# Attention with undivided probabilities, turned on TensorE by a product with a scaled unit matrix

## What is computed

```python
def memory_cross_attention(q_mem, k_mem, v_mem):
    s = jnp.einsum('bshd,bmhd->bhsm', q, k_mem).astype(jnp.float32) * (HEAD_DIM ** -0.5)
    p = jax.nn.softmax(s, axis=-1).astype(v_mem.dtype)
    return jnp.einsum('bhsm,bmhd->bshd', p, v_mem).reshape(B_, S_, MEM_W)

def forgetting_attention(q, k, v, c):
...
        s = jnp.einsum('bqhd,bkhd->bhqk', q[:, q0:q1], k[:, :q1]).astype(jnp.float32) * scale
        s = s + cT[:, :, q0:q1, None] - cT[:, :, None, :q1]
        causal = jnp.arange(q1)[None, :] <= jnp.arange(q0, q1)[:, None]
        s = jnp.where(causal, s, -jnp.inf)
        p = jax.nn.softmax(s, axis=-1).astype(v.dtype)
        outs.append(jnp.einsum('bhqk,bkhd->bqhd', p, v[:, :q1]))
```

## Time and profile before

| | us |
|---|---|
| runs of the kernel | 1977.71, 1978.26, 1981.58 |
| median | 1978.26 |
| span of the profiled execution (its own time is not shown beside it) | 1983.4 |
| PE busy | 1802.8 (91%) |
| DVE, ACT, POOL busy | 750.7, 385.6, 354.7 |
| attention of layer 0, first scores to last result | 198.7 to 285.4 |
| attention of layer 1, first scores to last result | 1149.75 to 1180.48 |

### The profile page before, as it was taken

One profiled execution on the slowest core, in us unless ns is written; L12 is line 12 of the kernel. 1 busy time (PEld: TensorE's weight loads), 2 busy tenths in 40 slices (PEclk: granted clock), 3 DMA queues, 4 the chain that ended last, 5 costly groups with the idle time before them and its releaser, 6 DMA issues. The chain is left out here.

```text
span 1983.4 us, 36215 instructions
## 1 busy us (share of the span) xinstructions
PE 1802.8 (91%) x12636; PEld 1111.3 (56%) x12637; DVE 750.7 (38%) x2168; ACT 385.6 (19%) x882; POOL 354.7 (18%) x450
## 2 busy tenths in 40 slices
PE   9999989889999988878899979999889999998777
PEld 7888434456666555543345438855456666664442
DVE  4221754723333223224255553425622333332225
ACT  2111650111111111102256143211011111110001
POOL 8452000011111111110012813200111111111110
PEclk9999999999999999998899978899999999999999
DMA  6220215599999999998123220015899999999997
GB/s 231 82 72 22 96 67 226 212 399 420 421 421 422 421 422 421 421 420 319 45 62 85 65 41 3 23 65 215 328 418 392 421 420 422 420 422 422 421 416 306
DMA packets 144184, 541.80 MB, mean 273 GB/s; under 512 B 31030, under 2 KB 68498, under 8 KB 94302
## 3 DMA queue, kind: packets, MB, share of 16 engines
q1 hardware_dynamic: 122782, 490.20, 61.7%
q0 software_dynamic: 21312, 50.37, 6.5%
HBM read 521.58 MB, written 46.14 MB: 286 GB/s over the span
## 5 line engine op out<-in xcount | busy, mean ns | idle before, releaser
L718 PE MATMUL bank<-W,XT 128*64 128x256 f32 x2880 | 325.9, 382 | 34.7 <-DMA W<-in_w_exp_up_dram 16.9
L718 PEld LDWEIGHTS bank<-W,XT 128*64 128x64 f32 x2880 | 233.7, 138 | 136.8 <-DMA W<-in_w_exp_gate_dram 24.2
L755 PE MATMUL bank<-W,ht 128*64 128x512 f32 x720 | 167.8, 608 | 14.0 <-DMA W<-in_w_exp_down_dram 9.2
L2235 PE MATMUL bank<-XT,room 128*128 128x512 f32 x352 | 158.2, 604 | 0.0
L729 DVE TENSOR_TENSOR sig<-sig,bank 128x256 f32<-128x256 f32 x72 | 30.4, 422 | 270.1 <-ACT sig L725 226.8
L718 PE MATMUL bank<-room,XT 128*64 128x256 f32 x864 | 101.5, 385 | 18.7 <-issue 10.0
L2235 PEld LDWEIGHTS bank<-XT,room 128*128 128x128 f32 x352 | 66.3, 193 | 82.6 <-issue 82.4
L784 POOL DMA_INDIRECT y_rows<-XT,row x36 | 36.4, 1012 | 421.1 <-DVE XT L777 421.1
L731 DVE TENSOR_TENSOR h<-sig,bank 128x256 f32<-128x256 f32 x72 | 30.4, 422 | 213.9 <-PE bank L718 213.9
L784 POOL DMA_INDIRECT y_rows<-y,row x36 | 36.8, 1021 | 413.7 <-DVE y L777 413.7
L704 ACT ACTIVATE XT<-bank 128x512 f32<-128x512 f32 x74 | 44.2, 597 | 328.8 <-PE bank L696 328.8
(11 more groups left out here) (490 smaller groups left out, 2802.9 us busy)
## 6 DMA issues: line engine op xcount, KB each, us to landing
W<-in_w_exp_gate_dram SPq DMA_DIRECT2D x88, 1024.0 KB
W<-in_w_exp_up_dram SPq DMA_DIRECT2D x88, 1024.0 KB
W<-in_w_exp_down_dram SPq DMA_DIRECT2D x88, 1024.0 KB
room<-in_w_exp_gate_dram SPq DMA_DIRECT2D x40, 1024.0 KB
third_high<-in_w_exp_down_dram SPq DMA_DIRECT2D x40, 1024.0 KB
W<-y_rows SPq DMA_DIRECT2D x24, 1024.0 KB, 13.6
third_up<-in_w_exp_up_dram SPq DMA_DIRECT2D x20, 1024.0 KB
w_shg<-in_w_exp_up_dram SPq DMA_DIRECT2D x20, 1024.0 KB
```

What stands on the lines that cost most here:

```text
L718: last = pe.matmul((gate, up)[m][64 * a:64 * a + 64, :], xt[s][:, k, 64 * a:64 * a + 64], weights(w, a, m)[:, k * FE:(k + 1) * FE], start= ...
L755: last = pe.matmul(B[5 + half][64 * a:64 * a + 64, :], ht[:, j, 64 * a:64 * a + 64], weights(w, a, 2)[:, at:at + 512], start=(j == 0), sto ...
L2235: last = pe.matmul(main(i)[:], wc[i % WBUFS][:, kb, :], K.XT[:, kb, :], start=(kb == 0), stop=(kb == KD - 1))
```

## The change

The scores, the maximum and the exponent stay. What was "divide, then transpose" becomes one product: the exponents of a block, undivided, are the weights, and what streams is the unit matrix with row q scaled by 1 / sum of row q. GpSimd makes this scaled unit matrix, 128 x 128, once per unit (`inverses`, four buffers). So the scaling on VectorE (layer 0) and on ScalarE (layer 1) goes, and so do the transpositions. In layer 0 VectorE copies the turned blocks of odd units (head e = 1) and ScalarE those of even ones; in layer 1 ScalarE copies all of them. TensorE's list is written by two units at a time: scores of units n and n + 1, turning of units n - 4 and n - 3 (`AHEAD` = 4), then two blocks of weighing. The rest of each list is put in the matching order.

```diff
-    BUFS, AHEAD = 4, 3
+    BUFS, AHEAD = 4, 4
...
+        for m in range(N):
+            s = m % BUFS
+            pool.wait_ge(inverted, m + 1)
+            if m >= BUFS:
+                pool.wait_ge(turned, m - BUFS + 1)
+            pool.tensor_scalar(inverses[s], K.ident[:], inv[:, s:s + 1], None, ALU.mult).then_inc(diagonal_made, 1)
...
         def turn(n):
-            pe.wait_ge(normed, n + 1)
+            pe.wait_ge(diagonal_made, n + 1)
             if n >= 2:
-                pe.wait_ge(kept, n - 1)
+                pe.wait_ge(kept[n % 2], n // 2)
             for b in range(n_blocks(n)):
-                last = pe.transpose(B[4 + n % 2][:, b * P:(b + 1) * P], prob[n % BUFS][:, b * P:(b + 1) * P], K.ident[:])
+                last = pe.matmul(B[4 + n % 2][:, b * P:(b + 1) * P], prob[n % BUFS][:, b * P:(b + 1) * P], inverses[n % BUFS],
+                                 start=True, stop=True)
...
-        for n in range(N + AHEAD + 2 + NT):
-            if n < N and n % 2 == 0:
+        for n in range(0, N + AHEAD + NT, 2):
+            if n < N:
                 scores(n)
-            j, b = divmod(n - AHEAD - 1, PER)
-            j -= 1
-            if 0 <= j and b < pair_blocks(j):
-                weigh(j, b)
             if AHEAD <= n < N + AHEAD:
                 turn(n - AHEAD)
+                turn(n + 1 - AHEAD)
+            j, b = divmod(n - AHEAD, PER)
+            j -= 1
+            if 0 <= j:
+                for block in range(b, min(b + 2, pair_blocks(j))):
+                    weigh(j, block)
...
+        for n in range(0, N + AHEAD, 2):
+            for i in (n, n + 1):
+                if i >= AHEAD and (i % 2 == 0 or bases is not None):
+                    keep(i - AHEAD)
+                if i < N:
+                    exponents(i)
...
+        for n in range(0, N, 2):
+            if n % PER == 0 and n >= 2 * PER:
+                leave(n // PER - 2)
+            for m in (n, n + 1):
+                for _ in range(2):
+                    next(pieces, None)
+                maximum(m)
+            if bases is None and n >= AHEAD:
+                keep(n + 1 - AHEAD)
+            invert(n)
+            invert(n + 1)
```

More of the change, by code:

```diff
@@ L1229, in fox_layer @@
     prob = [w_mem.rearrange("p k n -> p (k n)")[:, s * T:(s + 1) * T] for s in range(4)]
+    inverses = w_mem.rearrange("p k n -> p (k n)")[:, 4 * T:5 * T]
     x_sums = carve(P, (3 * HALF_K, HALF_T))
@@ L1499, in fox_layer @@
         with Phase(nc) as att_scope:
-            att = attention(K, L, att_scope, pairs, dict(qT=qT, kT=kT, v=v, sgT=sgT, qmT=qmT, probT=probT, prob=prob, bias=c_parts), w_out)
+            att = attention(K, L, att_scope, pairs, dict(qT=qT, kT=kT, v=v, sgT=sgT, qmT=qmT, probT=probT, prob=prob, inverses=inverses, bias=c_parts), w_out)
             with nc.Block() as block:
@@ L1631, in attention @@
     prob = d["prob"] if "prob" in d else [K.room_flat[:, taken + s * blocks * P:taken + (s + 1) * blocks * P] for s in range(BUFS)]
+    inverse_room = d["inverses"] if "inverses" in d else K.room_flat[:, taken + BUFS * blocks * P:taken + BUFS * (blocks + 1) * P]
+    inverses = [inverse_room[:, s * P:(s + 1) * P] for s in range(BUFS)]
     nmax = sb("nmax", [P, BUFS])
@@ L1634, in attention @@
     inv = sb("inv", [P, BUFS])
-    scored, maxed, exped, inverted, normed, turned, kept, weighed, out = (
-        sem(n) for n in ("scored", "maxed", "exped", "inverted", "normed", "turned", "kept", "weighed", "out"))
-    steps = sem("steps")
+    scored, maxed, exped, inverted, diagonal_made, turned, weighed, out = (
+        sem(n) for n in ("scored", "maxed", "exped", "inverted", "diagonal_made", "turned", "weighed", "out"))
+    kept = [sem("kept_even"), sem("kept_odd")]
     def n_blocks(n):
@@ L1696, in weigh @@
             if b == 0:
-                pe.wait_ge(kept, PER * (j + 1))
+                for e in range(2):
+                    pe.wait_ge(kept[e], NT * (j + 1))
                 if j >= 2:
@@ L1721, in tensor @@
         if first_chunk is not None:
-            pe.wait_ge(kept, N)
+            for e in range(2):
+                pe.wait_ge(kept[e], N // 2)
             pe.wait_ge(out, NP)
             first_chunk.products(pe)
-    def scalar(act):
[L1727 to L1748, removed]
@@ new lines, in turned_parts, with await_turned, keep, exponents @@
+    def turned_parts(m):
+        j, t, e = units[m]
+        nb = n_blocks(m)
+        return probT[j % 2][:, e, 0:nb, t * P:(t + 1) * P], B[4 + m % 2][:, 0:nb * P].rearrange("p (b q) -> p b q", b=nb)
+    def await_turned(eng, m):
+        j, t, e = units[m]
+        eng.wait_ge(turned, m + 1)
+        if j >= 2:
+            eng.wait_ge(weighed, j - 1)
+    def scalar(act):
+        def keep(m):
+            await_turned(act, m)
+            act.activation(*turned_parts(m), ACT.Copy).then_inc(kept[m % 2], 1)
+        def exponents(n):
+            act.wait_ge(maxed, n + 1)
+            if n >= BUFS:
+                act.wait_ge(turned, n - BUFS + 1)
+            w = P * n_blocks(n)
+            act.activation(prob[n % BUFS][:, 0:w], B[n % 4][:, 0:w], ACT.Exp, bias=nmax[:, n % BUFS:n % BUFS + 1],
+                           accum_out=total[:, n % BUFS:n % BUFS + 1]).then_inc(exped, 1)
+        for n in range(0, N + AHEAD, 2):
[4 more added lines that the diff above has]
+                    exponents(i)
@@ L1752, in vector @@
     def vector(dve):
-        step = Chain(dve, steps)
         def leave(j):
@@ L1762, in leave @@
                 dve.tensor_copy(K.XT[:, TOKW // P + i, :], o).then_inc(out, 1)
-        pieces = bases.solvers[1].pieces if bases is not None else iter(())
[L1765 to L1788, removed]
@@ L1789, in vector, with maximum, invert @@
-        for j in range(NP):
-            if PER * (j + 1) + AHEAD + 2 + NT > N:
-                leave(j)
+        def maximum(n):
+            dve.wait_ge(scored, n + 1)
+            if n >= BUFS:
+                dve.wait_ge(exped, n - BUFS + 1)
+            dve.tensor_reduce(nmax[:, n % BUFS:n % BUFS + 1], B[n % 4][:, 0:P * n_blocks(n)], AX.X, ALU.max,
+                              negate=True).then_inc(maxed, 1)
+        def invert(m):
+            s = slice(m % BUFS, m % BUFS + 1)
+            dve.wait_ge(exped, m + 1)
+            if m >= BUFS:
+                dve.wait_ge(diagonal_made, m - BUFS + 1)
+            dve.reciprocal(inv[:, s], total[:, s]).then_inc(inverted, 1)
@@ new lines, in keep @@
+        def keep(m):
+            await_turned(dve, m)
+            dve.tensor_copy(*turned_parts(m)).then_inc(kept[1], 1)
+        pieces = bases.solvers[1].pieces if bases is not None else iter(())
+        for n in range(0, N, 2):
[9 more added lines that the diff above has]
+            invert(n + 1)
@@ L1792, in vector @@
+        if bases is None:
+            for n in range(N, N + AHEAD, 2):
+                keep(n + 1 - AHEAD)
+        for _ in pieces:
+            pass
+        for j in range(NP - 2, NP):
+            leave(j)
         if bases is not None:
```

## The result

| | us |
|---|---|
| kernel before | 1979.76 median of 14 runs (1968.09 to 1987.64) |
| changed kernel | 1990.35 median of 14 runs (1986.1 to 1992.06) |
| ratio after / before | 1.0049, 95% interval 1.0034 to 1.0064 |

The change made the kernel slower by about 0.5%, some 10 us. The forecast was +2.5 us and its range ended at 1986.5.

The account below looks back on a forecast made before the run. TensorE was taken to bound layer 0's token pairs; layer 0's attention at +5.8 us and layer 1's at -3.3 gave +2.5 on the median 1978.26, so 1980.8 us, range 1975 to 1986.5.

Parts of the forecast that it names:

- Two passes, 0.22 us a block: Layer 0's turning: a plain f32 product is two records, 0.22 us a block for 0.11, +2.2 us a token pair.
- faster: Rival: in layer 0 the loop of dependent steps binds, not TensorE's list; waits go, about -8 us, 1970; chance 0.12.
- four times, not two: Rival: a plain FP32 product costs four times a transposition, 0.44 us a block; about +50, 2030 us; chance 0.02.
- The saving by the order, 0.98 us a pair: Layer 0's token pair: the 0.48 us wait goes, and four fewer switches between turning and weighing save 0.5 us.
- First memory pair +1.0: Layer 0, 260.94 to 270.41: 21 blocks turned cost 2.3 us more, less idle time, switches and the wait: +1.0 us.
- First pairs and drain, 0 each: Layer 0: first two token pairs 0 (-0.5 to +1) as TensorE waits already; drain's idle time covers 2.4 us: 0.
- GpSimd covered: Layer 0: GpSimd's scaled unit matrix, taken as 0.45 us per unit (far end 0.92), is hidden, costing nothing.
- GpSimd is on the way: Rival: GpSimd's step is 0.92 us or excludes VectorE; +1.5 layer 0, +2.7 layer 1 at most; 1982.8; chance 0.10.
- Layer 1's clock: Layer 1's attention: TensorE's clock rises after the first two steps, up by about 1163, as waits between products go.
- The clock stays low: Rival: layer 1 stays at half clock until the first weighing, +0.6 there, +6.4 in all, 1984.7; chance 0.14.
- Layer 1's four terms: Layer 1's attention: earlier scores -1.0, four two-unit steps -0.3, step with four weighings -1.2, drain -0.8; -3.3 us.

Follow-up runs that it names:

- places 1 / 60: Kernel before and changed kernel, each padded with jumped-over code so expert loops begin at places 1 (layer 0) and 60 (layer 1): 1976.63 and 1978.01 us.
- the control: Kernel before with jumped-over instructions moving TensorE's code by one whole 256-instruction piece, loops again at places 1 and 13: 1981.91 us, ratio 0.9996.

## Why the prediction was wrong

**The step that failed** is the sentence "What follows both stages starts behind them, so I carry their times to the end one to one". The sum for what it summed held. Carried over clean executions, layer 0's attention cost +6.0 us (forecast +5.8). Layer 1's gave between -1.8 (27.66 to 25.83) and -5.1 (29.9 to 24.8, places 1 / 60), its three changed profiles a mean of 25.3 and the seven with the old attention 29.0: -3.7 (forecast -3.3). That is +2.3 for the forecast's +2.5, and fits the differences at equal places, -0.4, +4.8 and +1.4 us. The other 8 us came from 300 to 370 more TensorE instructions ahead of two loops that they have nothing to do with: the kernel before, moved to the same places, lost as much (ratio 1.0042), and 7.0 us of it stand in layer 0's experts (548.8 us for 541.8 in the control). The prediction counted the added records as time on TensorE, and never as code to be fetched; it put what untouched stages lose by that at nothing, without a reason.

The Trainium skill has this mechanism ("Runtime: NRT & Kernel Launch", Instruction fetch mechanics): code comes in 16 KB blocks of 256 instructions, ahead of need and in sequence only, and a taken branch whose target isn't there has to wait for its block. The trace agrees: in layer 0 the jump took 0.29 to 0.38 us at places 1 and 3 and 5.5 to 6.2 us at four others, and every long one ended 2.3 to 2.5 us after a fetch had started. Weighed beforehand, it would have been a rival, with a price from the trace of the kernel before: the same jump took 4.21 us there in layer 1.

Point by point:

- *Two passes, 0.22 us a block: right.* PE's timeline of the changed kernel shows 16 records for 8 blocks and the products around them:

```profile
232.53 2.00 PE L1700 MATMUL bank<-W 128*128 128x128 f32 x16
234.47 0.92 PE L1685 MATMUL bank<-W 64*128 64x384 f32 x4
235.22 0.33 PE L1688 MATMUL bank<-c_parts,ones 64*128 64x384 bf16 x2
235.48 0.28 PE L1690 MATMUL bank<-causal,ident 128*128 128x128 bf16 x2
235.60 0.66 PE L1700 MATMUL bank<-W 128*128 128x128 f32 x4
236.19 1.73 PE L1715 MATMUL bank<-W 128*64 128x512 f32 x8
```

  From 232.53 to 234.47 are 1.94 us for 16 records, 0.12 each, and no row has an idle time. The token pair grew by 1.08 us (forecast 1.2). So the rival "faster" falls, since the waits did all go and the second pass still cost more; and "four times, not two" falls with it.
- *The saving by the order, 0.98 us a pair: right.* Layer 0 by transpositions with VectorE's old order took 9.49 us a pair for 10.43, which is 0.94 less, and the product in their place makes it 11.51, which is 2.02 more (forecast 2.2).
- *First memory pair +1.0: right* (10.68 for 9.47, +1.2). *First pairs and drain, 0 each: right only in sum.* Against the control the first two pairs gained 0.5 us and the drain lost 0.9.
- *GpSimd covered: right, at a higher price.* The source view of its step, and who waited:

```profile
L1668 POOL TENSOR_SCALAR W<-ident,att_inv x64: 604/605/631, 200.8 to 284.9; 128x128 f32<-128x128 f32 x64
...
  PEld bank L1700: 3.1, 9
```

  0.605 us for the 0.45 I took, between the ends that I gave. TensorE's weight loads waited for it 9 times, 3.1 us in all, never in the token pairs (four times from 264 us on, five in layer 1). The rival "GpSimd is on the way" falls.
- *Layer 1's clock: right, and earlier than forecast.* It was back at full by 1166.6 us after 10.2 us at half, for 17.1 before, with TensorE busy throughout from the first turning at 1163.22 on. The stage starts some 7 us later than in the trace of before, so the times compare from its start: 10.0 us into it, where the forecast's 1163 is 13.2 and the kernel before had 19.9. "The clock stays low" falls.
- *Layer 1's four terms: three near, one too small.* By the starts of PE's records in the two profiled executions they came to -1.1, -0.7, -1.4 and -1.6 us (forecast -1.0, -0.3, -1.2, -0.8). In the last, the drain, the kernel before had 3.4 us at half clock from 1176.45 on, so a part of that gain belongs to this execution.
- *The half clock in the rows it was read from.* The prediction's 86.7 us for layer 0 held some 10 us at half clock in its first pair and its drain; the stage was 3.4 us dearer than in the control (87.48 for 84.05, to the next stage's first product). The sum by differences survived this, since the steady pairs carried it; a sum of whole stage lengths would not have (91.46 less 87.48 gives +4.0).

## What to carry to other kernels

Adding instructions to an engine moves all its later code: where that engine later jumps in a loop while transfers are the bound, look at the branch's time in the source view and compare kernels at equal places of their code before a difference of 0.5% is put down to the edit. Pads of code that is jumped over, with a control of one whole piece, tell the two apart cheaply, and a good place may be worth more (12 us here) than the change itself. A product with a scaled unit matrix in place of divide and transpose pays where the engine that divides is the bound (layer 1), and costs where TensorE is (layer 0).

## What was not expected of the hardware

- **The price of a jump.** In layer 0 the long branch took 5.5 to 6.2 us while weights were streaming at 400 GB/s, once per loop. TensorE's hole was 5.05 us in the changed kernel and 5.22 in the moved one, half clock followed it, and layer 0's experts lost 6 to 7 us. Another jump of the same loop, at its first way in (L882), took 3.6 us before and 0.4 after the change, and doesn't show in the stage's length. After the first ways round the loop's branches took about 0.2 us, and from 470 to 900 us the instruction queue carried no packet in the changed kernel, so a loop of 1254 instructions stays in reach.
- **GpSimd and VectorE side by side.** The Trainium skill ("SBUF — State Buffer", Who interferes with whom) lets a VectorE instruction with two SBUF inputs wait for a GpSimd one that reads SBUF, and the earlier trace rows showed it with a select. In the changed kernel's layer 1 it did not happen beside the scaled unit matrices; the timeline of POOL and DVE:

```profile
1161.58 1.37 POOL L1668 TENSOR_SCALAR room<-ident,att_inv 128x128 f32<-128x128 f32 x2 [0.72 <-DVE att_inv L1795]
...
1162.35 0.21 DVE L1574 TENSOR_TENSOR W<-W 64x60 f32<-64x60 f32 x1
1162.60 0.18 DVE L1573 TENSOR_TENSOR W<-W 64x31 f32<-64x31 f32 x1
```

  The second scaled matrix ran up to 1162.95, and VectorE's products inside that time took 0.21 and 0.18 us, as before the change with GpSimd idle. Which operations of GpSimd exclude VectorE, these runs don't show.
- **Layer 1's loop at places 13 and 17** had jumps of 1.6, 4.2, 5.1, 6.0 and 6.2 us in five executions. In each a fetch was on its way: it started between 0.7 us before the branch and 3.8 us after it, and the branch ended 2.3 to 2.5 us behind that start. What sets the start, and why the good place there is 60 and not 1, stays open.
